# Down projections of a two-layer decoder kernel: 12 of 22 inner blocks as seven products of halves

## The reference, cut to what matters

```python
def _swiglu(h, wg, wu, wd):
    a = jnp.einsum('btd,df->btf', h, wg)
    b = jnp.einsum('btd,df->btf', h, wu)
    return jnp.einsum('btf,fd->btd', jax.nn.silu(a) * b, wd)
...
        xp = xp + g2p[:, None] * _swiglu(hp, w_ffn_gate[l], w_ffn_up[l], w_ffn_down[l])
        xs = xs + g2s[:, None] * _swiglu(hs, w_ffn_gate[l], w_ffn_up[l], w_ffn_down[l])
```

## Time and profile before

| | |
|---|---|
| median of 3 runs | 3023.31 us (3016.89 to 3028.66) |
| the profiled execution | 3026.01 us |
| its span, first to last instruction | 3024.1 us |
| granted clock of TensorE, mean | 0.979 |
| TensorE busy | 2881.4 us (95%) |
| VectorE, GpSimd, ScalarE busy | 1603.4, 1400.6, 940.6 us |
| HBM, mean over the span | 115 GB/s |

### The profile page before, as it was taken

One profiled execution on the slowest core, in us unless ns is written; L12 is line 12 of the kernel. 1 busy time (PEld: TensorE's weight loads), 2 busy tenths in 40 slices (PEclk: granted clock), 3 DMA queues, 4 the chain that ended last, 5 costly groups with the idle time before them and its releaser, 6 DMA issues. The chain is left out here.

```text
span 3024.1 us, 59642 instructions
## 1 busy us (share of the span) xinstructions
PE 2881.4 (95%) x24697; PEld 2678.1 (89%) x24697; DVE 1603.4 (53%) x2968; ACT 940.6 (31%) x1988; POOL 1400.6 (46%) x1273
## 2 busy tenths in 40 slices
PE   6999999996789999999999999999999999999998
PEld 4859999765689999999999999956699999999998
DVE  6399999556646644444345500066648544334435
ACT  3351111355533433332101311166525333332001
POOL 2122224463533877776334233144334777775333
PEclk9999999998899999999999999999999999999999
DMA  6726763642251122223322223163221221224222
GB/s 217 250 73 223 253 222 124 185 146 70 96 183 47 61 78 78 85 81 126 106 80 69 77 90 114 42 214 111 77 90 40 82 81 69 85 78 150 79 76 74
DMA packets 179181, 338.76 MB, mean 112 GB/s; under 512 B 21064, under 2 KB 94560, under 8 KB 177056
## 3 DMA queue, kind: packets, MB, share of 16 engines
q1 hardware_dynamic: 138576, 281.64, 27.4%
q10 hardware_dynamic: 40336, 53.31, 4.9%
HBM read 268.30 MB, written 79.49 MB: 115 GB/s over the span
## 5 line engine op out<-in xcount | busy, mean ns | idle before, releaser
L109 PE MATMUL tr_acc<-tr_quad_hi,ah_ring_hi 128*128 128x264 f32 x2432 | 694.5, 286 | 8.4 <-DVE tr_kept L1190 2.2
L111 PE MATMUL tr_acc<-tr_quad_hi,ah_ring_lo 128*128 128x264 f32 x2432 | 692.7, 285 | 0.0
L110 PE MATMUL tr_acc<-tr_quad_lo,ah_ring_hi 128*128 128x264 f32 x2432 | 690.2, 284 | 0.0
L577 POOL TENSOR_TENSOR ah_ring_lo<-ah_raw,ah_ring_hi 128x512 fp32r<-128x512 f32 (+1 forms) x402 | 554.8, 1386 | 159.1 <-ACT ah_ring_hi L920 146.2
L109 PEld LDWEIGHTS tr_acc<-tr_quad_hi,ah_ring_hi 128*128 128x128 f32 x2432 | 458.6, 189 | 10.6 <-DVE tr_kept L1190 2.6
L110 PEld LDWEIGHTS tr_acc<-tr_quad_lo,ah_ring_hi 128*128 128x128 f32 x2432 | 458.7, 189 | 0.1
L111 PEld LDWEIGHTS tr_acc<-tr_quad_hi,ah_ring_lo 128*128 128x128 f32 x2432 | 458.2, 188 | 0.0
L575 POOL CAST ah_ring_hi<-ah_raw 128x512 fp32r<-128x512 f32 (+1 forms) x162 | 102.9, 635 | 528.9 <-PE tr_acc L111 464.6
L109 PE MATMUL tr_acc<-tr_part_hi,ah_ring_hi 128*128 128x352 f32 x1038 | 335.6, 323 | 2.0 <-DVE tr_kept L1228 2.0
L110 PE MATMUL tr_acc<-tr_part_lo,ah_ring_hi 128*128 128x352 f32 x1038 | 332.9, 321 | 0.0
L111 PE MATMUL tr_acc<-tr_part_hi,ah_ring_lo 128*128 128x352 f32 x1038 | 332.6, 320 | 0.0
(11 more groups left out here) (391 smaller groups left out, 6418.8 us busy)
## 6 DMA issues: line engine op xcount, KB each, us to landing
f_ada_w<-in_w_ada_dram SPq DMA_DIRECT2D x48, 1024.0 KB, 5.6
scratch_inner<-tr_kept ACTq DMA_DIRECT2D x88, 264.0 KB, 2.2
tr_staged<-scratch_inner SPq DMA_DIRECT2D x44, 528.0 KB, 4.3
ah_raw<-in_w_gate_dram SPq DMA_DIRECT2D x44, 512.0 KB, 3.5
ah_raw<-in_w_up_dram SPq DMA_DIRECT2D x44, 512.0 KB, 4.5
ah_raw<-in_w_down_dram SPq DMA_DIRECT2D x64, 256.0 KB, 3.6
f_raw<-in_w_dram SPq DMA_DIRECT2D x24, 512.0 KB, 7.5
out_z_dram<-f_stage ACTq DMA_DIRECT2D x60, 176.0 KB, 1.9
```

Source lines behind the costliest of these rows:

```text
L109: pe.matmul(out, w_hi, hi, start=start, stop=False)
L110: pe.matmul(out, w_hi, lo, start=False, stop=False)
L111: return pe.matmul(out, w_lo, hi, start=False, stop=stop)
L577: pool.tensor_tensor(lo[:, 0:width], own, hi[:, 0:width].bitcast(F32), ALU.subtract).then_inc(w_ready, 1)
```

## The change

The parts become 4, 4, 3, 4, 4 and 3 blocks. Parts 1, 3 and 4, with 12 of the 22 blocks, are done by sevenths: left factor, a unit's weights of 4 inner by 2 output blocks, in four quarters of 2 x 1 blocks; right factor, 4 inner blocks by 1056 tokens, in four quarters of 2 blocks by 528 columns (an "eighth" of a full inner set). The left columns are the first 496 prompt tokens and the 32 samples, in two halves of 248 + 16; the right ones are the other 528 prompt tokens. A unit then takes seven products (`DOWN_ORDER`) of 2 blocks x 2 pieces of 264 columns x 3 passes = 12 matmuls (`seventh`). M6, M7 and M4 accumulate onto the bank that M1 began, M3 onto that of M5, and VectorE adds the bank to the residual after each product (`seventh_residual`), so each partial sum goes where it belongs as it arises. M4 of a unit comes after M5 of the next one. The plain parts keep their steps.

The mixtures of the inner blocks are VectorE's (three a part, in two halves) and GpSimd's (one); upper halves are ScalarE's, lower ones VectorE's, in two halves of 528 columns each, hung behind steps or products of the part before (`rest_after`, `upper_after`). The mixtures of the weights (four a unit) and their lower halves (seven, 256 columns) are GpSimd's, their upper halves ScalarE's. A unit of sevenths takes seven places of the ring of six. The staging buffer is gone: loads go to where the lower halves will lie. SyncE waits for whole parts (`place_free`) before units `DOWN_FIRST` + 2, 5, 9, 13 and 17; those waits and loads stand ahead of that unit's weights in its queue.

```diff
-TRUNK_PARTS = [4, 4, 4, 4, 3, 3]
+TRUNK_PARTS = [4, 4, 3, 4, 4, 3]
 assert sum(TRUNK_PARTS) == KF
 PART_FIRST = [sum(TRUNK_PARTS[:p]) for p in range(len(TRUNK_PARTS))]
 PART_MAX = max(TRUNK_PARTS)
+SEVENTHS = (1, 3, 4)
...
+DOWN_ORDER = [M1, M5, M6, M3, M2, M7, M4]
+LEFT = HALF - (N - T)
+LEFT_TOKENS, LEFT_SAMPLES = LEFT // 2, (N - T) // 2
+EIGHTH = 2 * HALF
...
+            if u in self.split_no:
+                run = [v for v in range(u, end) if all(w in self.split_no for w in range(u, v + 1))]
+                for v in run:
+                    for n, product in enumerate(DOWN_ORDER[:6]):
+                        if n == 2 and v > u:
+                            self.events += [("product", v - 1, M4), ("read", v - 1, M4)]
+                            order.append((v - 1, M4))
+                        self.events += [("product", v, product), ("read", v, product)]
+                        order.append((v, product))
+                self.events += [("product", run[-1], M4), ("read", run[-1], M4)]
+                order.append((run[-1], M4))
+                u = run[-1] + 1
+            elif last and u == end - KD // 2:
...
+                self.bank[u, t] = {M5: 1, M3: 1, M2: 2}.get(t, 3 * (self.split_no[u] % 2))
+                self.free_after[u, t] = held.get(self.bank[u, t])
...
-        self.slots += [(u, i) for u in range(DOWN_FIRST, end) for i in range(2)]
+        self.slots += [(u, i) for u in range(DOWN_FIRST, end) if u not in self.split_no for i in range(2)]
+        for u in self.split_units[::-1]:
+            if u + 1 not in self.split_no:
+                at = 1 + max(i for i, (v, _) in enumerate(self.slots) if v < u)
+                self.slots[at:at] = [(v, DOWN_ORDER.index(product)) for v, product in order
+                                     if v <= u and all(w in self.split_no for w in range(v, u + 1))]
...
+        rest_items = [("mix", M5, 0), ("mix", M5, 1), ("mix", M6, 0), ("mix", M6, 1), ("rest", M1, 0), ("rest", M1, 1),
+                      ("mix", M4, 0), ("mix", M4, 1)] + [("rest", q, h) for q in DOWN_ORDER[1:] for h in range(2)]
+        upper_after, rest_after = {}, {}
+        for p in range(len(TRUNK_PARTS) - 1):
+            host = [at for what, *at in events if what in ("mm", "product") and (at[0] - DOWN_FIRST) // 4 == p
+                    and DOWN_FIRST <= at[0] < plan.z_first]
+            if p + 1 in SEVENTHS:
+                if p in SEVENTHS:
+                    where = [2 + i for i in range(20)]
+                    uppers = [4, 6, 8, 10, 12, 15, 17]
+                else:
+                    where = [2 + p // 2 + i * (10 - p // 2) // 20 for i in range(20)]
+                    uppers = [2 + p // 2 + i for i in range(7)]
+                for i, item in enumerate(rest_items):
+                    rest_after.setdefault(tuple(host[where[i]]), []).append((p + 1, item))
+                for i, q in enumerate(DOWN_ORDER):
+                    upper_after.setdefault(tuple(host[uppers[i]]), []).append((p + 1, q))
+            else:
+                for k in range(TRUNK_PARTS[p + 1]):
+                    upper_after.setdefault(tuple(host[7 + 6 * k]), []).append((p + 1, k))
+                    for h in range(2):
+                        rest_after.setdefault(tuple(host[9 + 6 * k + 3 * h]), []).append((p + 1, ("part", k, h)))
...
+        def place_free(eng, p, early=False):
+            if p == 0:
+                eng.wait_ge(made[1], 7 * (KF // 2 - 2) + 2)
+            elif p == 1:
+                eng.wait_ge(made[1], 7 * (KF // 2 - 1))
+            elif p == 2:
+                part_over(eng, 0)
+            elif p == 3:
+                part_over(eng, 1)
+            elif p == 4:
+                part_over(eng, 1 if early else 2)
+            else:
+                part_over(eng, 3)
...
+            def left_load(p, q, kh):
+                for k in range(2):
+                    f = PART_FIRST[p] + 2 * kh + k
+                    stored_inner(f)
+                    dst = eighth_raw[p, q][:, k].rearrange("p (b n) -> p b n", b=2)
+                    sp.dma_start(dst[:, :, 0:LEFT_TOKENS], io["inner"][f][:, 0:LEFT].rearrange("p (b n) -> p b n", b=2)
+                                 ).then_inc(eighth_in[p, q], 16)
+                    sp.dma_start(dst[:, :, LEFT_TOKENS:BLOCK], io["inner"][f][:, T:N].rearrange("p (b n) -> p b n", b=2)
+                                 ).then_inc(eighth_in[p, q], 16)
+            def right_load(p, q, kh):
+                f = PART_FIRST[p] + 2 * kh
+                stored_inner(f + 1)
+                sp.dma_start(eighth_raw[p, q][:], io["inner"][f:f + 2, :, LEFT:T].rearrange("k p n -> p k n")).then_inc(eighth_in[p, q], 16)
+            def eighth_loads(p, first, rest):
+                if first:
+                    place_free(sp, p, True)
+                    left_load(p, M1, 0)
+                    right_load(p, M7, 0)
+                    right_load(p, M3, 1)
+                if rest:
+                    place_free(sp, p)
+                    left_load(p, M2, 1)
...
-                if DOWN_FIRST <= u < plan.z_first and (u - DOWN_FIRST) % 4 == 1:
-                    p = (u - DOWN_FIRST) // 4
-                    if p == 0:
-                        part_loads(0)
-                    if p + 1 < len(TRUNK_PARTS):
-                        part_loads(p + 1)
+                if u == DOWN_FIRST + 1:
+                    part_loads(0)
+                elif u == DOWN_FIRST + 2:
+                    eighth_loads(1, True, True)
+                elif u == DOWN_FIRST + 5:
+                    part_loads(2)
+                elif u == DOWN_FIRST + 9:
+                    eighth_loads(3, True, True)
+                elif u == DOWN_FIRST + 10:
+                    eighth_loads(4, True, False)
+                elif u == DOWN_FIRST + 13:
+                    eighth_loads(4, False, True)
+                elif u == DOWN_FIRST + 17:
+                    part_loads(5)
...
+            def seventh_factor(u, n):
+                v, b = plan.split_no[u], u % 2
+                r11, r12, r21, r22 = (down_factor(u, DOWN_ORDER.index(q)) for q in (M1, M2, M7, M4))
+                mix = w_sum[b][:, 0:2 * P]
+                if n == 0:
+                    loaded(pool, u)
+                split(u, n, down_factor(u, n))
+                if n == 0:
+                    if v >= 2:
+                        pool.wait_ge(w_ready, plan.slot_no[plan.split_units[v - 2], DOWN_ORDER.index(M3)] + 1 - AHEAD)
+                    pool.tensor_tensor(mix, r21, r22, ALU.add).then_inc(factor_mix, 1)
+                    pool.wait_ge(factor_mix, 4 * v + 1)
+                    pool.tensor_tensor(r21, r11, r21, ALU.subtract).then_inc(factor_mix, 1)
+                elif n == 1:
+                    pool.wait_ge(w_ready, plan.slot_no[u, 1] + 1 - AHEAD)
+                    pool.wait_ge(factor_mix, 4 * v + 2)
+                    pool.tensor_tensor(r11, mix, r11, ALU.subtract).then_inc(factor_mix, 1)
+                    pool.wait_ge(factor_mix, 4 * v + 3)
+                    pool.tensor_tensor(mix, r12, r11, ALU.subtract).then_inc(factor_mix, 1)
+                    pool.wait_ge(factor_mix, 4 * v + 4)
+            def mix_seventh(p):
+                place_free(pool, p, True)
+                eighth_landed(pool, p, M3)
+                for h in range(2):
+                    mixed(pool, p, M5, h)
+                    own = eighth_raw[p, M7][:, h]
+                    pool.tensor_tensor(own, eighth_raw[p, M3][:, h], own, ALU.subtract).then_inc(eighth_mix7, 1)
...
+            def seventh(u, product):
+                p, n = seventh_of(u), DOWN_ORDER.index(product)
+                bank_free(u, product)
+                weights_ready(pe, plan.slot_no[u, n])
+                if units[u][1] == 0:
+                    pe.wait_ge(eighth_ready, 14 * place_no(p) + 2 * n + 2)
+                w_hi_s, w_lo_s = slot(u, n)
+                out, fresh = pair[plan.bank[u, product]], product in (M1, M2, M5)
+                for b in range(2):
+                    for k in range(2):
+                        of = slice(P * k, P * k + P)
+                        upper, lower = (v[p, product][:, k, BLOCK * b:BLOCK * b + BLOCK] for v in (eighth_hi, eighth_lo))
+                        done = passes(pe, out[:, b, 0:BLOCK], w_hi_s[:, of], w_lo_s[:, of], upper, lower, fresh and k == 0, k == 1, not fresh)
+                done.then_inc(product_done, 1)
...
+            def eighth_half(p, product):
+                if product == M1:
+                    place_free(act, p, True)
+                elif product == M5:
+                    place_free(act, p)
+                if product in (M1, M2, M3):
+                    eighth_landed(act, p, product)
+                elif product == M7:
+                    act.wait_ge(eighth_mix7, 2 * place_no(p) + 2)
+                else:
+                    mixed(act, p, product, 1)
```

(64 more changed lines are left out.)

203 lines of the change are left out of this document (134 added, 69 removed).

## The result

The changed kernel takes 3057.98 us (median of 4 runs, 3053.35 to 3061.64); the kernel before, beside it on the same chip, 3023.97 (4 runs, 3016.89 to 3028.66). The ratio is 1.0114 with an interval of 1.0089 to 1.0138: slower by 34 us, 33 us above the forecast of 3025 and 8 us beyond the upper end of the range. The profiled execution spans 3054.8 us against 3024.1, so 30.7 of it can be followed in the two traces.

A forecast was written before the change was run, and what follows sets the result against it. TensorE's matmul count times spacing was taken to bound the down phase. Per layer -15.0 + 2.6 + 2.2 + 5.5 + 5 + 0.5 = +0.8, +1.6 us in two layers, giving about 3025 us; eight-in-ten range 2998 to 3050.

The forecast's parts named there:

- B: Unit DOWN_FIRST + 9, after part 1: weights queued behind ten inner loads; TensorE stalls 2.2 us (1 to 3.5).
- A: Unit DOWN_FIRST + 5, in part 1: weights queued behind inner loads make M4 late; stall 2.6 us (1 to 4).
- C: Unit DOWN_FIRST + 17, waiting for part 3: same loads as A, M4 wanted sooner; stall 5.5 us (4 to 7).
- -15.0 on TensorE: Down phase: 1008 matmuls of 264 columns replace 864 of 352, saving 15.0 us a layer.
- DOWN_FIRST + 13: At this unit: four DMAs, then weights; M4 ready at 11.3 us against 11.7 wanted, so no stall.
- the cycle between: Other seventh units: weights wait for GpSimd's M4 rest; cycle 10.2 us, just TensorE's 10.2; no cost, no reserve.
- R2: Rival: access shared by VectorE and GpSimd decides, D is 14 and the weights' cycle lengthens; 3043 us, chance 0.25.
- D: Parts 3 and 4: VectorE's items, slowed beside GpSimd, delay its bank reads; 5 us a layer (0 to 14).
- The start of the phase: Wait before the first down matmul, while VectorE makes part 0's lower halves: priced at nothing.
- The clock: Lower granted clock after idling, with C's stall in pieces: 0.5 us a layer (0 to 2).
- R3: Rival: durations count or accumulating onto a read bank costs, TensorE gains nothing and stalls remain; 3051 us, chance 0.02.

The follow-up runs named there:

- e8: Against the changed kernel: unit weights issued first, second unit's weights held at the start, late VectorE items, M7 before M2 in a run's last unit; 3010.64 us.
- e1: Against the changed kernel: before units DOWN_FIRST + 5, 9, 10, 13 and 17 SyncE issues weights before waiting and loading inner blocks; 3033.23 us.
- e7: Against e1: in the last unit of each run of sevenths M7 comes before M2, so M4 no longer follows M7 directly; 3024.07 us.
- e5: Against the changed kernel: GpSimd's four weight mixtures of each seventh unit cut to 2 columns, results not the reference's; 3047.72 us.
- e2: Against the changed kernel: SyncE holds unit DOWN_FIRST + 1's weights until VectorE has made all lower halves of part 0; 3050.92 us.
- e3: Against the changed kernel: the edits of e1 and e2 together; 3020.37 us, ratio 0.9990 to the kernel before.
- e4: Against the changed kernel: 7 of VectorE's 20 preparing operations per seventh part left out, results not the reference's; 3052.37 us.

## Why the prediction was wrong

Its frame held: a gain of 15.0 us a layer on TensorE, stalls of the same size against it, and the places of three of them. What failed is the sum on the other side: 29.6 us in layer 0 and 28.4 in layer 1, where I had 15.8. Over both layers the errors are 7.1 us for the clock, 5.3 for VectorE's reads, 5.3 for the wider spacing, 4.8 for the start, 4.5 for B, 2.7 for GpSimd's weights cycle, and -3.3 for A and C. By its own terms:

- **-15.0 on TensorE.** Right in matmuls and spacing (121.3 ns in a clean run). About 2.4 to 2.9 us a layer go to a spacing slightly wider than that over the whole phase, which I had not counted; 1.9 to 2.1 remain in e8, when nearly all waits are gone. Its cause is open.
- **A, 2.6.** 1.4 and 2.3: within its bounds.
- **B, 2.2 (1 to 3.5).** 4.4 and 4.5, outside. The step that failed is "2.1 us + bytes at 0.36 MB/us" with 2.6 MB of bytes. SyncE was held for 6.2 us by ten issues of about 0.4 to 0.5 us, two of them taking 2.07 together, and the 0.4 us an issue of the earlier trace rows I had not added up. But the DMA engines were full from 1507.8 on: they moved 0.5 MB more than I had counted, and at 282 GB/s in the first full stretch. Which of the two set the landing is open.
- **C, 5.5.** 4.7 and 4.5: within its bounds.
- **`DOWN_FIRST + 13`, nothing, and the cycle between, "nothing now, but no reserve".** The product M4 that I priced had no wait. But the same late load left GpSimd without a pause from 1552.7 on, and in layer 0 TensorE waited 1.0 and 1.7 us for halves at M5 of the third unit and M4 of the second. So the cycle did lengthen past 10.2 us there, as the second half of R2's argument says, though not in layer 1 and not in the other units. In e1, where these weights are issued ahead of the loads, the two waits are gone.
- **D, 5 (0 to 14).** 8.1 and 7.2. Part 3's start was placed and sized right (2.7 predicted; 3.1, and 4.2 without B's stall in front). Inside part 3 I had 2.9 and VectorE's reads cost 0.7 and 1.3. Missing were the ends of both runs, where M4 is written right behind M7 and its bank is not yet read: 1.1 us each, shown by e7, where a reordering removes them, some 0.7 in part 1, and in layer 0 a wait of 1.3 in part 4. The price of an item, 0.85 to 0.91, was right for rests (0.898) and low for mixtures (1.189); e5 shows that GpSimd's mixtures lengthen both.
- **The start of the phase, nothing.** 3.0 and 1.8, and the half clock behind it. This term was not in the sum. The prediction moved weights in SyncE's queue but followed only those that came later, not the unit whose weights came earlier. It did not ask what an earlier landing sets off. e2 shows it.
- **The clock, 0.5 (0 to 2).** 2.9 and 5.2. The largest error in sum. I had taken C's broken stall as the only candidate. Six stretches came, up to 1.5 us each, behind the first wait in both layers, behind B in both, and behind two waits of parts 3 and 4 in layer 1.

The median is 33 us above the forecast and the profiled execution 29.1 above its own (3056.7 against 3027.6). The terms above make 26.4 of these 29.1, 1.7 lie outside the changed code, and 1.0 is in no term.

R2, slower at 3043, was the nearest of the rivals. Its price was too low and its mechanism only part of the cause: by e1 the queue's order in parts 1 to 4 accounts for 24.7 of the 34 us (its down phases are 12.1 and 12.6 us shorter than the changed kernel's, 24.7 in sum as well: 21.8 of waits A, B and C, 2.7 of GpSimd's, 1.8 of clock, the rest spacing, against 3.0 more of waits for VectorE), and by e3 queue order and start together for 37.6. One price in the prediction is a slip: R3 leaves the stalls at 15.8 a layer, not 13.8, which makes 3055 and not 3051.

Not settled: the wider spacing; which part of B's landing is issue and which transfer; and the 5.4 us between the down phases, where the code is the same. Of these 2.2 are one wait for GpSimd, here first in the changed kernel, then in the one before:

```profile
2022.40 1.97 PE L2769 MATMUL pc_turn<-ident,pc_prob 128*128 128x128 f32 x8 [5.28 <-POOL pc_prob L2702]
```

```profile
2008.84 1.43 PE L2473 MATMUL pc_turn<-ident,pc_prob 128*128 128x128 f32 x8 [3.04 <-POOL pc_prob L2406]
```

Around its end the changed kernel has a stretch at half clock that the kernel before has not:

```profile
2021.20:2024.60 3.40, 2.20 (x12) 1.82 (x14) 0.20 (x1) 1.05 (x2) 3.26 (x5) 0.50 0.27 103
```

## What to carry to other kernels

In an in-order DMA queue, put what the bottleneck needs next ahead of anything that waits for the bottleneck; here this alone was 25 of 34 us. Count the issues of a burst, and the bytes that are queued behind it as well. Read for each wait which engine ended last: taking work from one engine pays only until the next one is late (e4). When a load is moved, follow what its earlier landing sets off as well as what is late: a load brought forward can cost as much as one held back. Price a stall of some microseconds with the clock behind it, and look for the place of an operation that shares an access before looking for a cheaper operation.

## What the runs showed of the hardware

- A 528-column operation with two SBUF inputs takes 0.69 us alone and up to 1.84 beside GpSimd, whose own 512-column operation goes from 1.31 to 1.63. Of eight in a row (7.63 us; 5.03 alone in e2) the three beside GpSimd took 1.79, 1.11 and 1.79, the five beside DMA transfers 0.69 each.
- Two DMA issues in one row took 2.07 us on SyncE while the others in the burst took 0.38 to 0.47 each. In e1's run the same pair took 1.52, and a like pair in the burst at the start of the phase 0.92. I had expected issue times to be even.
- Stalls of one length do not cost one price: after the same 3.0 us of idling at part 3's start the clock fell in layer 1 (2912.1) and not in layer 0 (1552).
